# A mixer, router and mixture of experts on one core: last tile's first output blocks moved ahead, routing masks in pairs of tiles

## The reference

```
h = h + jnp.concatenate([a, s], axis=-1) @ w_out[i]          # (512,1024) @ (1024,1024)
h = h + hierarchical_moe(rmsnorm(h, g_ffn[i]), ...)

def hierarchical_moe(v, grp_w, grp_b, exp_w, exp_b, w_gate, w_up, w_down):
    grp_prob = softmax(tf @ grp_w + grp_b)                   # 4 groups
    grp_p, grp_idx = lax.top_k(grp_prob, 1)                  # the best group
    exp_logits = einsum('td,gde->tge', tf, exp_w) + exp_b    # 8 experts in each group
    sel_logits = take_along_axis(exp_logits, grp_idx...)     # those of the best group
    top_w, top_idx = lax.top_k(softmax(sel_logits), 2)       # the two best experts in it
    ...
    for g in range(4):                                       # 32 experts, 256 hidden units each
        hg = silu(t @ w_gate[g]) * (t @ w_up[g])             # 1024 -> 256, twice
        hg = hg * combine[:, g]
        out = out + hg @ w_down[g]                           # 256 -> 1024
```

## Time and profile before

| what | value |
|---|---|
| median of three runs | 515.67 us |
| the profiled execution: its time, its span | 516.12 us, 514.2 us |
| busy share of the span: TensorE, VectorE, ScalarE, GpSimd | 93%, 45%, 33%, 29% |
| moved by DMA | 144.73 MB, mean 281 GB/s |
| mean granted TensorE clock | 0.981 |
| chain that ended last: TensorE, DMA | 74%, 16% |

### The profile page before, as it was taken

One profiled execution on the slowest core, in us unless ns is written; L12 is line 12 of the kernel. 1 busy time (PEld: TensorE's weight loads), 2 busy tenths in 40 slices (PEclk: granted clock), 3 DMA queues, 4 the chain that ended last, 5 costly groups with the idle time before them and its releaser, 6 DMA issues.

```text
span 514.2 us, 7264 instructions
## 1 busy us (share of the span) xinstructions
PE 479.3 (93%) x2718; PEld 265.4 (52%) x2718; DVE 232.1 (45%) x683; ACT 169.9 (33%) x283; POOL 150.8 (29%) x136
## 2 busy tenths in 40 slices
PE   3899999999999999989999999987999987999993
PEld 3445555744854457655555555543454543444441
DVE  2799958999233258642222222220211111564525
ACT  5633676547442333111111111120212111214464
POOL 1059999714100001222223222220120210003350
PEclk9899999999999999989999999998999998999997
DMA  8774300399499986899999999999999996990022
GB/s 297 145 202 93 69 0 1 122 158 176 148 346 410 421 345 220 320 382 396 421 418 417 419 416 414 421 417 420 421 418 420 416 408 227 394 375 2 0 82 82
DMA packets 60139, 144.73 MB, mean 281 GB/s; under 512 B 27586, under 2 KB 36838, under 8 KB 47816
## 3 DMA queue, kind: packets, MB, share of 16 engines
q1 hardware_dynamic: 54504, 133.92, 70.9%
q0 software_dynamic: 5328, 10.31, 5.2%
q10 hardware_dynamic: 272, 0.04, 0.0%
HBM read 138.17 MB, written 14.19 MB: 296 GB/s over the span
## 4 chain that ended last, share of the span: by engine, by line
PE 74%; DMA 16%; issue 3%; ACT 3%; DVE 2%; SPq 1%; DVEq 0%; POOLq 0%
PE bank L1653 67%; DMA ring<-in_exp_w_up_dram 6%; DMA big<-in_exp_w_up_dram 6%; PE bank L2059 2%; DMA moe<-v_d,gidx_all 2%; DMA h<-in_x_dram 1%; SPq L364 1%; PE bank L1753 1%; PE bank L2078 1%; PE bank L1743 1%; ACT L558 1%; PE bank L1916 1%; PE bank L2176 1%; ACT moe L550 0%; ACT moe L554 0%
## 5 line engine op out<-in xcount | busy, mean ns | idle before, releaser
L1653 PE MATMUL bank<-ring,moe 128*64 128x256 f32 (+2 forms) x848 | 112.6, 411 | 5.1 <-DMA ring<-in_exp_w_up_dram 4.7
L1653 PEld LDWEIGHTS bank<-ring,moe 128*64 128x64 f32 x848 | 61.3, 140 | 42.3 <-issue 14.6
L1579 POOL DMA_INDIRECT pairs_d<-moe,sidx_all x32 | 31.8, 994 | 156.5 <-PE bank L2059 79.3
L922 DVE TENSOR_TENSOR vrow<-moe,bank 64x128 f32<-64x128 f32 x64 | 18.6, 291 | 120.4 <-ACT moe L821 119.4
L1653 PE MATMUL bank<-ut,big 128*128 128x512 f32 x128 | 59.1, 610 | 2.2 <-ACT ut L562 2.2
L821 ACT ACTIVATE moe<-bank 64x256 f32<-64x256 f32 x32 | 12.1, 378 | 139.6 <-PE bank L1653 139.6
L550 ACT ACTIVATE moe<-bank 128x512 f32<-128x512 f32 (+1 forms) x65 | 36.5, 582 | 60.6 <-PE bank L1653 50.5
L1653 PE MATMUL bank<-ring,ut 128*128 128x512 f32 x128 | 55.7, 593 | 0.4 <-DVE ut L922 0.4
L1653 PE MATMUL bank<-big,moe 128*64 128x256 f32 (+1 forms) x264 | 43.5, 443 | 2.6 <-DMA big<-in_exp_w_up_dram 2.3
L922 DVE TENSOR_TENSOR ring<-ring,bank 128x64 f32<-128x64 f32 (+1 forms) x142 | 39.5, 278 | 2.8
L1653 PEld LDWEIGHTS bank<-ut,big 128*128 128x128 f32 x128 | 24.1, 195 | 29.4 <-issue 28.1
(11 more groups left out here) (198 smaller groups left out, 630.0 us busy)
## 6 DMA issues: line engine op xcount, KB each, us to landing
ring<-in_exp_w_gate_dram SPq DMA_DIRECT2D x19, 1024.0 KB
ring<-in_exp_w_down_dram SPq DMA_DIRECT2D x18, 1024.0 KB, 23.1
ring<-in_exp_w_up_dram SPq DMA_DIRECT2D x17, 1024.0 KB
big<-in_exp_w_up_dram SPq DMA_DIRECT2D x7, 1024.0 KB
big<-in_exp_w_down_dram SPq DMA_DIRECT2D x7, 1024.0 KB, 32.0
big<-in_exp_w_gate_dram SPq DMA_DIRECT2D x6, 1024.0 KB
ut<-in_exp_w_up_dram SPq DMA_DIRECT2D x4, 1024.0 KB
h<-in_exp_w_down_dram SPq DMA_DIRECT2D x4, 1024.0 KB
```

The costliest lines, as they stand in the source:

```text
L922: return dve.tensor_tensor(o, a, b, op)
L1579: pool.indirect_dma_start(pairs, bass.IndirectOffsetOnAxis(ap=index, axis=0), at(moe, ALL, M_Y + k * 512, [[1, 512]]), None, bounds_check= ...
L1653: return pe.matmul(o, a, b, start=start, stop=stop, skip_group_check=loose)
```

## The change

It has four parts.

1. TensorE does chunks 4 and 5 of blocks 6 and 7 (the last tile's two halves) between the transposes of tiles 0 and 1, and their chunks 6 and 7 behind block 5. The matmuls are the same in number. `part`, `fold` and the transposes stand between other blocks than before; `fold(2)` goes to bank 4 and stands behind the last transposes.
2. SyncE asks for piece 14 when six blocks are done, 15 and 21 when eight are.
3. ScalarE copies the parts of tiles 0 and 1 behind tile 1's scaling, that of tile 2 between the two squares of tile 3.
4. VectorE makes the masks for tiles 0 and 1, and then for tiles 2 and 3, with one function; the fused chain of the last tile is gone. The ranks and `X1` go by the same pairs. `rank(1)` has a third matmul, and `picked(2)` now waits for the second `X1` too.

```diff
-        H_BANK, LOG_BANK = (0, 2, 4, 2), (1, 3, 5, 2)
+        H_BANK, LOG_BANK = (0, 2, 4, 2), (1, 3, 4, 2)
...
             sp.wait_ge(cat_done, NB)
             for p in range(6, 12):
                 weights(sp, p)
+            sp.wait_ge(wo1_ps, 6)
+            weights(sp, 14)
             sp.wait_ge(wo1_ps, 2 * NT)
-            for p in (14, 15, 21):
+            for p in (15, 21):
                 weights(sp, p)
...
-                if t == NA - 1:
-                    for k in range(NA):
-                        part_out(k)
                 scaled_rows(t)
+                if t == 1:
+                    part_out(0)
+                    part_out(1)
             t = NA
             act.wait_ge(h_done, 2 * NT - 1)
             mean_root(at(h, ALL, t * DM, [[1, 512]]), at(moe, ALL, M_XT, [[1, 512]]), S_HALF, 0, half_in)
+            part_out(2)
...
             norm(0)
             turned(0)
-            residual(4)
-            residual(5)
             norm(1)
             turned(1)
-            turned(2)
-            norm(2)
             logits(0)
             logits(1)
-            logits(2)
-
...
+            def masks(t0, between=None):
+                one, four, eight = [[1, 2]], [[4, 2], [1, 4]], [[NEG, 2], [1, NEG]]
+                te = [[NE, 2], [NEG, NG], [1, NEG]]
+                l4 = at(logit, ALL, 36 * t0, [[36, 2], [1, 4]])
+                le = at(logit, ALL, 36 * t0 + 4, [[36, 2], [NEG, NG], [1, NEG]])
+                def v(name, dims):
+                    width = {"g1": 4, "goh": 4, "pr": NE, "px": NE, "M1": NE, "M2": NE, "MS": NE,
+                             "gm": 1, "g2": 1, "m1": 1, "q2": 1, "m2": 1, "q4": 1}
+                    return qv(name, dims, t0 * width.get(name, NEG))
+                def first_best(src, best, a, b, hot):
+                    peak(v(best, one), v(src, eight))
+                    seq(tt(v(a, eight), v(src, eight), v(best, [[1, 2], [0, NEG]]), ALU.is_equal))
+                    seq(tt(v(a, eight), v(a, eight), cv(C_LOW, [[0, 2], [1, NEG]]), ALU.mult))
+                    peak(v(b, one), v(a, eight))
+                    seq(tt(v(hot, eight), v(a, eight), v(b, [[1, 2], [0, NEG]]), ALU.is_equal))
+                dve.wait_ge(logit_sb, t0 + 2)
+                peak(v("gm", one), l4)
+                seq(tt(v("g1", four), l4, v("gm", [[1, 2], [0, 4]]), ALU.is_equal))
+                seq(tt(v("g1", four), v("g1", four), cv(C_LOW, [[0, 2], [1, 4]]), ALU.mult))
+                peak(v("g2", one), v("g1", four))
+                seq(tt(v("goh", four), v("g1", four), v("g2", [[1, 2], [0, 4]]), ALU.is_equal))
+                seq(tt(v("pr", te), v("goh", [[4, 2], [1, 4], [0, NEG]]), le, ALU.mult))
+                peak(v("sel", eight), v("pr", [[NE, 2], [1, NEG], [NEG, NG]]), ALU.add)
+                first_best("sel", "m1", "q1", "q2", "oh1")
+                if between:
+                    between()
+                seq(pick(v("s2", eight), v("oh1", eight), -3.0e38, v("sel", eight), ALU.mult, ALU.add))
+                first_best("s2", "m2", "q3", "q4", "oh2")
+                seq(tt(v("s2", eight), v("oh1", eight), v("oh2", eight), ALU.add))
+                both = tt(v("MS", te), v("goh", [[4, 2], [1, 4], [0, NEG]]), v("s2", [[NEG, 2], [0, NG], [1, NEG]]),
+                          ALU.mult)
+                if t0 == 0:
+                    seq(both)
+                    own.do(dve.memset(qv("px", [[1, NE]]), 0.0))
+                    seq(dve.tensor_copy(qv("px", [[1, NE]], NE), qv("MS", [[1, NE]])))
+                    tt(qv("px", [[1, NE]], 2 * NE), qv("MS", [[1, NE]]), qv("MS", [[1, NE]], NE), ALU.add
+                       ).then_inc(mask_done, 1)
                 else:
-                    ins.then_inc(mask_done, 1)
+                    both.then_inc(mask_done, 1)
+                for k in (1, 2):
+                    own.do(tt(v(f"M{k}", te), v("goh", [[4, 2], [1, 4], [0, NEG]]),
+                              v(f"oh{k}", [[NEG, 2], [0, NG], [1, NEG]]), ALU.mult))
...
+            masks(0, lambda: residual(4))
+            residual(5)
+            residual(6)
+            turned(2)
+            norm(2)
             dve.wait_ge(half_in, 1)
             dve.tensor_scalar(at(small, ALL, S_HALF, [[1, 1]]), at(small, ALL, S_HALF, [[1, 1]]), 1.0 / DM, EPS, ALU.mult,
                               ALU.add).then_inc(half_root, 1)
             residual(7)
             turned(NA)
-            first_pair(0, NA)
+            first_pair(0, 2)
             norm(NA)
+            logits(2)
             logits(NA)
-
-            def last(name, dims, width):
-                return qv(name, dims, NA * width)
-
...
-            peak(m1, sel)
-            seq(pick(q1, sel, m1, low8, ALU.is_equal, ALU.mult))
-            peak(q2, q1)
-            seq(dve.tensor_scalar(oh1, q1, q2, None, ALU.is_equal))
-            seq(pick(s2, oh1, -3.0e38, sel, ALU.mult, ALU.add))
-            peak(m2, s2)
-            seq(pick(q3, s2, m2, low8, ALU.is_equal, ALU.mult))
-            peak(q4, q3)
-            seq(pick(s2, q3, q4, oh1, ALU.is_equal, ALU.add))
-            pick(last("MS", ge, NE), last("g1", [[1, 4], [0, NEG]], 4), g2, last("s2", [[0, NG], [1, NEG]], NEG),
-                 ALU.is_equal, ALU.mult).then_inc(mask_done, 1)
-            own.do(dve.tensor_scalar(goh, g1, g2, None, ALU.is_equal))
-            own.do(dve.tensor_scalar(oh2, q3, q4, None, ALU.is_equal))
+            masks(2)
+            dve.wait_ge(mask_done, 2)
+            first_pair(2, 2)
             own.settle()
...
-            tt(last("d4", [[1, 4]], 4), l4, last("gm", [[0, 4]], 1), ALU.subtract).then_inc(d4_done, 1)
+            tt(qv("d4", [[4, NT], [1, 4]]), at(logit, ALL, 0, [[36, NT], [1, 4]]), qv("gm", [[1, NT], [0, 4]]), ALU.subtract
+               ).then_inc(d4_done, 1)
...
             def rank(part):
 
                 pe.wait_ge(mask_done, part + 1)
+                total = bank[5][:, NT * NE:(NT + 1) * NE]
                 if part == 0:
-                    mm(bank[5][:, 0:NA * NE], at(cst, ALL, C_TRI, [[1, P]]), at(moe, ALL, Q["MS"], [[1, NA * NE]]),
+                    mm(bank[5][:, 0:2 * NE], at(cst, ALL, C_TRI, [[1, P]]), at(moe, ALL, Q["MS"], [[1, 2 * NE]]),
                        True, False, True)
-                    mm(bank[5][:, 0:NT * NE], at(cst, ALL, C_ONE, [[1, P]]), at(moe, ALL, Q["px"], [[1, NT * NE]]),
+                    mm(bank[5][:, 0:3 * NE], at(cst, ALL, C_ONE, [[1, P]]), at(moe, ALL, Q["px"], [[1, 3 * NE]]),
                        False, False, True)
-                    got = mm(bank[5][:, NT * NE:(NT + 1) * NE], at(cst, ALL, C_ONE, [[1, P]]),
-                             at(moe, ALL, Q["px"] + NA * NE, [[1, NE]]), False, False, True)
+                    got = mm(bank[5][:, 3 * NE:5 * NE], at(cst, ALL, C_ONE, [[1, P]]),
+                             at(moe, ALL, Q["px"] + 2 * NE, [[0, 2], [1, NE]]), False, False, True)
                 else:
-                    mm(bank[5][:, NA * NE:NT * NE], at(cst, ALL, C_TRI, [[1, P]]), at(moe, ALL, Q["MS"] + NA * NE, [[1, NE]]),
-                       False, False, True)
-                    got = mm(bank[5][:, NT * NE:(NT + 1) * NE], at(cst, ALL, C_ONE, [[1, P]]),
-                             at(moe, ALL, Q["MS"] + NA * NE, [[1, NE]]), False, True, True)
+                    mm(bank[5][:, 2 * NE:4 * NE], at(cst, ALL, C_TRI, [[1, P]]),
+                       at(moe, ALL, Q["MS"] + 2 * NE, [[1, 2 * NE]]), False, False, True)
+                    mm(bank[5][:, 3 * NE:5 * NE], at(cst, ALL, C_ONE, [[1, P]]),
+                       at(moe, ALL, Q["MS"] + 2 * NE, [[0, 2], [1, NE]]), False, False, True)
+                    got = mm(total, at(cst, ALL, C_ONE, [[1, P]]), at(moe, ALL, Q["MS"] + 3 * NE, [[1, NE]]),
+                             False, True, True)
                 got.then_inc(rank_ps, 1)
 
             def picked(t):
 
-                pe.wait_ge(x1_done, 1 if t < NA else 2)
+                pe.wait_ge(x1_done, 1 if t < 2 else 2)
                 pe.wait_ge(v_done, t + 1)
                 for j in range(KC):
                     got = mm(bank[j // 4 * 6][:, (j % 4) * P:(j % 4 + 1) * P], at(h, ALL, t * DM + j * P, [[1, P]]),
...
 
                 wout(n, n, range(4, 8)).then_inc(wo1_ps, 1)
 
-            def wout1_folded(n):
+            def wout1_part(n, chunks):
 
                 t, half = n // 2, n % 2
-                for c in range(4, 8):
-                    last = mm(bank[n][:, :], at(ut, ALL, c * T + t * P, [[1, P]]),
-                              at(big, ALL, c * DM + half * 512, [[1, 512]]), c == 4, c == 7)
-                    if c == 4:
-                        for k in range(NA):
-                            fold(k)
-                last.then_inc(wo1_ps, 1)
+                for c in chunks:
+                    got = mm(bank[n][:, :], at(ut, ALL, c * T + t * P, [[1, P]]),
+                             at(big, ALL, c * DM + half * 512, [[1, 512]]), c == 4, c == 7, True)
+                return got
 
```

(34 more changed lines are left out.)

38 lines of the change are left out of this document (removed).

## The result

Over 20 runs each the changed kernel took 516.73 us (median) and the kernel before 514.55 us; the ratio is 1.0043, 95% interval 1.0032 to 1.0054, so 2.2 us slower (1.6 to 2.8). The forecast was +1.55 us. The times of each kernel spread over 3.8 us.

What follows compares the result with a forecast made beforehand. The prediction took the weight stream as the bound, its time set by expert 0's start. Its terms, -0.40 + 0.90 + 1.05 = +1.55 us, against the 515.67 us median gave 517.2 us; 8 in 10: 514.3 to 519.8 us.

Steps and rivals of the forecast that it cites:

- The stream bounds the kernel, and its length doesn't change: Expert stage: the saturated DMA stream of 96 weight pieces limits; the end follows the start of expert 0 one to one.
- A piece asked for earlier is worth 0: SyncE's queue: piece 14 asked for 6.5 us earlier gains 0, bounds -2.5 us and 0.
- TensorE up to the last logits, -0.4 us: TensorE from tile 0's transposes to the last logits: they end at 199.48 us in place of 199.88 us, -0.4 us.
- The last mask chain, +0.9 us: VectorE's last masks: 20 dependent steps in place of 15, 4.45 us against 3.55 us, +0.9 us.
- rank(1) and the wait, +1.05 us: TensorE from rank(1) to picked(2), which now waits for two tiles' X1: 1.52 us in place of 0.47 us, +1.05 us.
- Sum, +1.55 us at the start: Start of expert 0 on TensorE: 209.9 us in place of 208.32 us, +1.55 us.
- the wait ahead of `picked(2)`: Sign in the profile after: TensorE idle for 0.8 us ahead of picked(2), waiting for X1.
- that for the masks: Sign in the profile after: TensorE idle for about 1.4 us ahead of rank(1), waiting for the masks.
- The end moves by more than the start: Sign named ahead that would show the prediction wrong: the kernel's end moving by more than expert 0's start.
- The second slow stretch: Rival, TensorE's clock: new waits bring another drop ahead of picked(2), about 1.76 us, 519.0 us; chance 0.22.
- The first gap counts: Rival, DMA engines: asking for piece 14 early gives its 2.5 us of transfer, 513 us, faster; chance 0.10.
- the chain hides: Rival, last mask chain: logits come 2 us earlier, start unmoved or up to 1 us earlier, 514.7 to 515.7 us; chance 0.16.

Runs made afterwards that it cites:

- ten steps: Kernel before with ten more dependent reductions in the last tile's mask chain; ratio 1.0078 (1.0047 to 1.0108), +4.0 us, six runs.
- twenty steps: Kernel before with twenty more dependent reductions in the last tile's mask chain; ratio 1.0107 (1.0085 to 1.0128), +5.5 us, five runs.
- experiment 5: Changed kernel with pieces 14, 15 and 21 all asked for only when picked(1) is done; ratio 1.0037 (1.0018 to 1.0055) to the kernel before, +1.9 us.
- experiment 4: Changed kernel with piece 14 asked for together with 15 and 21, when all eight blocks are done; ratio 1.0034 (1.0015 to 1.0053) to the kernel before.
- experiment 3: Changed kernel with ScalarE's square of the last tile's first half ahead of tile 2's scaling; ratio 1.0026 (1.0009 to 1.0044) to the kernel before, +1.35 us.
- Experiment 7: Kernel before with the last tile's mask chain unfused, 20 steps in place of 15, run twice; ratios 0.9986 and 1.0000.
- experiment 6: Kernel before with one more wait: picked(2) also waits for the last tile's X1; ratio 1.0011 (0.9995 to 1.0028), +0.6 us.
- Experiment 2: Kernel before with only masks, ranks and X1 by pairs of tiles; ratio 1.0038 (1.0022 to 1.0054), +2.0 us.
- experiments 1 to 5 and 10: 1: changed kernel again, no edit, ratio 1.0031. 10: changed kernel with half square first and table of tokens ahead of expert 0, ratio 1.0016. Both to the kernel before.

## Why the prediction was right, point by point

- **The stream bounds the kernel, and its length doesn't change.** Right. The stream took 215.0 us before, 214.3 us after, 214.1 us with ten and with twenty steps, and TensorE first waited for weights at 331 us or later in every profile. From the start to the last waiting step it took 219.6 to 220.5 us in ten of the twelve kernels that begin with expert 0, whether the start was 0.5 or 5.6 us later than before. The other two are before (220.9 us) and experiment 5 (221.0 us). That is the step from start to end of the prediction, shown to about 0.5 us.
- **A piece asked for earlier is worth 0.** Right: experiment 4, and experiment 5, where 15 us later cost at most about 0.8 us.
- **TensorE up to the last logits, -0.4 us.** Wrong in size: +0.08 us. The transposes of tile 2 began 16.56 us behind those of tile 0, where 16.23 us had been worked out, and the chain from there to VectorE's step on the half tile took 4.75 us (190.74 to 195.49 us), not 4.4 us:

```profile
192.23 1.29 DVE L925 TENSOR_TENSOR moe<-bank,vec 128x512 f32<-128x512 f32 x2 [0.60 <-PE bank L1895]
...
195.49 0.15 DVE L1237 TENSOR_SCALAR small<-small 128x1 f32<-128x1 f32 x1 [1.90 <-ACT moe L556]
```

  The 0.35 us of this are a longer wait of VectorE for the transposes: its copy began 1.49 us behind their start, where those of tiles 0 and 1 began 1.14 and 1.20 us behind. Why, the runs don't show. Of the two delays, 0.7 us together, 0.2 us came back between that step and the first picked product (3.23 us; the prediction has 3.43 us). That the chain over ScalarE's half square sets this place is shown by experiment 3: it gave 0.65 us back at the start.
- **The last mask chain, +0.9 us.** 0.64 us. The 20 steps took 4.32 us to `rank(1)` (199.22 to 203.54 us), 0.13 us less than worked out, against 3.61 us before (200.45 to 204.06 us), where 3.55 us had been put in; that is 0.71 us, and the chain began 0.07 us sooner behind the first picked product. Experiment 7 gives 0.47 us for the unfused form alone with one tile. The prediction's reason for the price of a step doesn't hold: it takes 0.07 us as an estimate and lays the rest of the 0.22 us to the waits between the steps. In the rows each step is itself busy for 0.16 to 0.18 us, and 0.03 to 0.05 us lie between two. The price was taken from the trace, so the sum didn't suffer.
- **rank(1) and the wait, +1.05 us.** 1.18 us: from `rank(1)` to the ranks' step it took 0.97 us (203.54 to 204.51 us), where 0.84 us had been worked out. The wait alone is 0.85 us (experiment 6).
- **Sum, +1.55 us at the start.** +1.93 us, and +2.2 us (1.6 to 2.8) in the times. Two terms were too small by 0.5 and 0.1 us, one too large by 0.3 us: that the sum is off by 0.4 us and not by 0.6 us is luck. Experiment 2 puts the loss in the pairs.
- **The signs.** Of the signs named ahead, the wait ahead of `picked(2)` came out (0.79 us for 0.8 us), that for the masks was shorter (1.00 us for 1.4 us), and piece 14 and the DMA engines behaved as told. "The end moves by more than the start" isn't shown: 1.93 us lie inside the interval of the times.
- **The rivals.** The second slow stretch is real: of the seven profiles of kernels with pairs (the six of experiments 1 to 5 and 10, and the changed kernel's own) two had it on the products behind the last `X1` (1.6 us on the path), two on the products ahead of the waits (0.4 us); of the six of kernels with tile 3's masks made alone and no added steps or ten, none had one there. It falls in some executions of one kernel and not in others, so it isn't a case beside the forecast but a share of its average. How large a share isn't shown. Over 80 runs of the changed kernel and of experiments 1 to 5 the mean granted clock is 0.9859, over 93 runs of before 0.9862, so in the mean hardly any slow time was added; more likely stretches fell here in place of elsewhere. The wait for the masks, which looks like pure loss, also takes up most of a stretch that falls ahead of it. "The first gap counts" is out by experiment 4, and "the chain hides" by the start, 1.93 us later.

## What to carry to other kernels

Look for the moment from which a saturated stream runs, and price a change by what it does to that moment: filling an idle stretch of the DMA engines ahead of it is worth nothing when the places for data, not the engines, are what is full. Splitting tiles 2 + 2 in place of 3 + 1 puts two tiles' work behind the last one's result; what could hide behind another tile's product no longer does. Work that produces addresses for a gather can be worth moving ahead of work that doesn't depend on it: here it gave 1.3 us (0.5 to 2.2), on one kernel.

## What the runs showed of the hardware

The spread of the times is mostly TensorE's clock: over 93 runs of the kernel before, made beside the experiments, a straight line in the mean granted clock accounts for two thirds of the variance. The levels that hold most of the runs, and the highest that holds more than two:

```
clock 0.981: 19 runs, mean 515.8 us      clock 0.988: 16 runs, mean 514.3 us
clock 0.984: 14 runs, mean 515.0 us      clock 0.991: 13 runs, mean 513.4 us
clock 0.987: 11 runs, mean 514.6 us      clock 0.994:  4 runs, mean 512.3 us
```

The steps of 0.003 fit single stretches at 1.2 GHz: one adds 1.6 to 1.7 us to its group (5.39 to 7.08 us, 3.82 to 5.45 us), which is 0.0033 of the span. The profile of before (0.981) has four, at 18, 226, 356 and 430 us, and that of the changed kernel (0.994) has none of these; both have a slow clock in the last 10 us, as all the profiles do. 3.5 us lie between the ends of the list, over 0.013 of clock; the line has 2.3 us for 0.01. In the profiles such stretches stood behind waits of TensorE, at 18, 200, 206, 226, 340, 356 or 430 us, but not behind each in each execution: with 2.3 us of waiting ahead of it the group at 429 us took 7.08 us in the profile of before and 5.39 us, behind 2.4 us, in that of the changed kernel. A single profile against a single profile was off by 3.9 us here (-1.7 us in the spans, +2.2 us in the times).

The line gives an estimate of what each kernel costs at equal clock: its runs and those of before beside it are both taken as distances from the line, about which single runs scatter by 0.64 us. It takes out the clock whether or not the edit caused it. In us over before:

| kernel | at the start, profile | at the end, times | at equal clock |
|---|---|---|---|
| changed (20 runs; the 93 of before) | 1.9 | 2.2 | 1.9 ± 0.3 |
| changed again (1) | 2.3, with a slow stretch | 1.6 | 1.9 ± 0.4 |
| pairs alone (2) | 3.3, 1.7 without the slow stretch | 2.0 | 2.0 ± 0.4 |
| half square first (3) | 1.3 | 1.3 | 1.2 ± 0.4 |
| piece 14 with the others (4) | 1.9 | 1.8 | 1.5 ± 0.4 |
| all three late (5) | 2.3, with a slow stretch | 1.9 | 2.4 ± 0.4 |
| one more wait (6) | 0.85 | 0.6 | 1.0 ± 0.4 |
| unfused, twice (7) | 0.5, 0.5 | -0.7, 0.0 | 0.0, 0.1 ± 0.4 |
| ten steps, twenty steps (8) | 2.0, 5.6 | 4.0, 5.5 | 3.3, 4.7 ± 0.6 |

By it the end of the changed kernel follows its start one to one, to 0.3 us. Two rows don't fit so well: the unfused chain, lower at the end than at the start by about the interval, and ten steps, higher by more than it.
